# A two-layer hybrid decoder in split float32: p turns moved apart, low parts of the output weights in halves, first halves of the output product around the last head, and turns moved in the gated embedding

## What is computed

```python
for i in range(DEPTH):                                   # DEPTH = 2
    x = layer_norm(DN_ALPHA * x + 0.5 * swiglu(x, gate[i, 0], up[i, 0], down[i, 0]), ...)
    m = mixer_attention(...) if i % 2 == 0 else mixer_sgu(...)
    x = layer_norm(DN_ALPHA * x + m, ...)
    x = layer_norm(DN_ALPHA * x + 0.5 * swiglu(x, gate[i, 1], up[i, 1], down[i, 1]), ...)
    x = x + jax.nn.sigmoid(x @ ple_w_gate[i]) * (p[i] @ ple_w_proj[i])
# mixer_attention: h = x @ w_in; 8 heads with a relative-position bias and 8 "forgetting" heads
# (logits + c_t - c_s, c = cumsum(log_sigmoid(f))); softmax; o = concat(heads); return o @ w_out
```

## Time and profile before

| | us |
|---|---|
| median of three runs (1066.32 to 1066.38) | 1066.37 |
| profiled execution | 1067.42 |
| its span | 1065.1 |
| TensorE busy | 1033.4 |
| VectorE busy | 611.2 |
| ScalarE busy | 449.7 |
| POOL busy | 39.2 |

### The profile page before, as it was taken

The page is one execution under the profiler, slowest core; times in us unless marked ns, Lnnn a source line. Parts: engine busy times, 40 slices in busy tenths (PEclk is TensorE's granted clock), DMA queues, the critical chain, the costliest instruction groups (busy, mean ns, idle before and its releaser), DMA issues.

```text
span 1065.1 us, 12659 instructions
## 1 busy us (share of the span) xinstructions
PE 1033.4 (97%) x4770; PEld 845.3 (79%) x4770; DVE 611.2 (57%) x706; ACT 449.7 (42%) x523; POOL 39.2 (4%) x53
## 2 busy tenths in 40 slices
PE   7999999999998899999998999999999899999998
PEld 6888888777877688888886888888887688888886
DVE  5645455874455855445576554545677775454574
ACT  5434444245444443434435344344344354444441
POOL 2000000100000100000010000000110100000010
PEclk9999999999998999999999999999999999999999
DMA  8865655445133585565636755556267575655531
GB/s 287 280 203 184 203 189 167 136 142 157 40 103 111 184 275 197 160 205 182 201 105 219 261 181 180 197 159 208 87 207 237 174 261 188 206 187 168 197 119 40
DMA packets 129218, 191.46 MB, mean 180 GB/s; under 512 B 5368, under 2 KB 95480, under 8 KB 129056
## 3 DMA queue, kind: packets, MB, share of 16 engines
q1 hardware_dynamic: 126256, 180.37, 51.4%
q0 software_dynamic: 2928, 10.61, 3.0%
HBM read 189.90 MB, written 1.06 MB: 179 GB/s over the span
## 4 chain that ended last, share of the span: by engine, by line
PE 88%; DVE 4%; DMA 3%; ACT 2%; issue 2%; SPq 0%; POOL 0%; ACTq 0%; DVEq 0%
PE gu L358 19%; PE gu L360 18%; PE gu L359 18%; PE acc L358 9%; PE acc L360 9%; PE acc L359 9%; PE tp L416 4%; DVE g_lo L992 1%; ACT g_hi L742 1%; PE acc L561 1%; DMA rawB<-in_ffn_w_up 1%; DMA v_att<-bias_rows 1%; DMA rawB<-in_sgu_w_out 1%; DVE xT_lo L992 1%; DMA ws_tok<-in_sgu_w_s 0%
## 5 line engine op out<-in xcount | busy, mean ns | idle before, releaser
L358 PE MATMUL gu<-g_hi,xT_hi 128*128 128x512 f32 x928 | 365.3, 394 | 7.7 <-DVE xT_lo L992 7.5
L360 PE MATMUL gu<-g_hi,xT_lo 128*128 128x512 f32 x928 | 362.3, 390 | 0.0
L359 PE MATMUL gu<-g_lo,xT_hi 128*128 128x512 f32 x928 | 361.9, 390 | 0.0
L358 PEld LDWEIGHTS gu<-g_hi,xT_hi 128*128 128x128 f32 x928 | 174.7, 188 | 45.8 <-DVE xT_lo L992 7.4
L360 PEld LDWEIGHTS gu<-g_hi,xT_lo 128*128 128x128 f32 x928 | 174.6, 188 | 36.7
L359 PEld LDWEIGHTS gu<-g_lo,xT_hi 128*128 128x128 f32 x928 | 174.8, 188 | 35.6 <-issue 0.2
L791 ACT ACTIVATE stage<-gu 128x256 f32<-128x256 f32 x88 | 33.8, 384 | 380.1 <-PE gu L360 380.1
L992 DVE TENSOR_TENSOR g_lo<-rawA,g_hi 128x2048 fp32r<-128x2048 f32 (+1 forms) x64 | 143.4, 2240 | 82.9 <-ACT g_hi L742 82.9
L992 DVE TENSOR_TENSOR g_lo<-rawB,g_hi 128x2048 fp32r<-128x2048 f32 (+1 forms) x64 | 143.1, 2237 | 25.1 <-ACT g_hi L742 25.1
L1091 DVE SCALAR_TENSOR_TENSOR stage<-stage,gu 128x256 f32<-128x256 f32 x88 | 37.0, 421 | 197.0 <-ACT stage L791 197.0
L358 PE MATMUL acc<-d_hi,hT_hi 128*128 128x512 f32 x352 | 144.4, 410 | 0.0
(11 more groups left out here) (167 smaller groups left out, 682.8 us busy)
## 6 DMA issues: line engine op xcount, KB each, us to landing
rawD<-in_ffn_w_down SPq DMA_DIRECT2D x44, 1024.0 KB, 4.9
rawA<-in_ffn_w_gate SPq DMA_DIRECT2D x43, 512.0 KB, 4.0
rawA<-in_ffn_w_up SPq DMA_DIRECT2D x43, 512.0 KB, 5.0
rawB<-in_ffn_w_gate SPq DMA_DIRECT2D x43, 512.0 KB, 4.2
rawB<-in_ffn_w_up SPq DMA_DIRECT2D x43, 512.0 KB, 5.4
rawA<-in_attn_w_in SPq DMA_DIRECT2D x12, 512.0 KB, 4.6
rawB<-in_attn_w_in SPq DMA_DIRECT2D x12, 512.0 KB, 4.7
rawA<-in_ple_w_gate SPq DMA_DIRECT2D x8, 512.0 KB, 4.7
```

Of the source, the lines that this page charges most:

```text
L358: pe.matmul(dst, hi[b], w_hi[b], start=first and b == 0, stop=False)
L359: pe.matmul(dst, hi[b], w_lo[b], start=False, stop=False)
L360: done = pe.matmul(dst, lo[b], w_hi[b], start=False, stop=last and b == len(hi) - 1)
```

## The change

Four edits, made together.

- ATTN_ORDER: p turn 0 goes ahead of k's turn ("turn", 1, 1), p turn 1 behind the product ("g", 3, 0), ahead of head 0, on every engine.
- Heads: VectorE's two low parts of 4 blocks of the output weights become four of 2 blocks, in heads 12 to 15 behind the logits, each for the high part that ScalarE made a head earlier; a semaphore `out_high_front` tells of the first halves. On TensorE the probabilities' turn goes ahead of the attention result's turn; ScalarE's and VectorE's steps for that turn move from heads 16 and 17 to heads 15 and 16.
- Output product: the first part of (0, 0) runs ahead of head 17 (the last values), the first part of (0, 1) behind it; then both oT turns, and the loop does only second parts for j = 0. VectorE makes the low part of the next load (`lo_g(g0 + 8, 0)`) ahead of the xT_lo of turn 0, and that of the FFN's first half (`lo_g(g0 + 9, 0)`) ahead of the second residual of half 0. ScalarE's high part for it waits for `out_front_done` in place of the end of (0, 1).
- Gated embedding of layer 0: TensorE does the half-1 turns six products before the end of product 1, and product 2 in two parts, each behind its own bank. ScalarE does half 1's high parts ahead of sigmoid 1 and the high part of the next load ahead of sigmoid 2, behind `ple_front_done`. VectorE does half 1's low parts behind the first gate product. In the FFN behind it ScalarE and VectorE do half 1 ahead of the weights' parts of the next chunk.

```diff
@@ -55,13 +55,14 @@
...
 ("g", 1, 0), ("turn", 0, 1), ("exp",), ("g", 1, 1), ("turn", 1, 0), ("log",),
-("g", 2, 0), ("turn", 1, 1), ("pT", 0), ("pT", 1), ("g", 2, 1), ("cT",),
-("g", 3, 0), ("head", 0), ("g", 3, 1), ("turn", 3, 0), ("head", 1), ("head", 2),
+("g", 2, 0), ("pT", 0), ("turn", 1, 1), ("g", 2, 1), ("cT",),
+("g", 3, 0), ("pT", 1), ("head", 0), ("g", 3, 1), ("turn", 3, 0), ("head", 1), ("head", 2),
 ("g", 4, 0), ("turn", 3, 1), ("head", 3), ("head", 4),
...
 ("g front", 5, 1), ("head", 9), ("g back", 5, 1), ("head", 10),
-] + [("head", n) for n in range(HEADS + 3, 2 * HEADS + 2)] + [("oT", 0), ("oT", 1)]
+] + [("head", n) for n in range(HEADS + 3, 2 * HEADS + 1)] + [
+("out front", 0), ("head", 2 * HEADS + 1), ("out front", 1), ("oT", 0), ("oT", 1)]

@@ -251,6 +252,8 @@
...
 proj_full, proj_taken = sem("proj_full"), sem("proj_taken")
+out_high_front, out_front_done, ple_front_done = (
+sem("out_high_front"), sem("out_front_done"), sem("ple_front_done"))
 ws_loaded, vn_ready, mix_done, sgu_bias_ld, ws_raw = (
@@ -524,14 +527,25 @@
...
                 pe.wait_ge(act_done, a0 + n - 1)
-            if n % 2 == 0:
+            if n == 0 or n == 2 and i == 1:
                 xT_wait(h, use)
...
                 ln_turn(0, x0, (t0, t0 + 1))
-            g_product(g0 + j, (g0 + j) % 2, h, gu[j][:, :])
-            if n == 1:
+            if n == 1 and i == 0:
+                for part, ks in ((0, 4), (1, 6)):
+                    pe.wait_ge((split_a, split_b)[part], g0 + j)
+                    g_piece((g0 + j) % 2, h, gu[j][:, :], 4 * part, ks)
                 half1()
+                g_piece((g0 + j) % 2, h, gu[j][:, :], 6, KB).then_inc(g_done, 1)
+            elif n == 2 and i == 0:
+                for part in range(2):
+                    pe.wait_ge(tp_taken[part], use[h] + 1)
+                    done = g_piece((g0 + j) % 2, h, gu[j][:, :], 4 * part, 4 * part + 4)
+                    done.then_inc((ple_front_done, g_done)[part], 1)
+            else:
+                g_product(g0 + j, (g0 + j) % 2, h, gu[j][:, :])
             if n == 1 and i == 1:
+                half1()
                 d_product(d0, d0 % 2, 0, pT_hi[:, 0], pT_lo[:, 0], first=True, last=True)
@@ -648,6 +662,8 @@
...
                     scores(n)
+                if 1 <= n <= 2 * HEADS:
+                    probs_turn(n - 1)
                 if n in (15, 16):
@@ -655,30 +671,29 @@
...
                     done.then_inc(o_turned, 1)
-                if 1 <= n <= 2 * HEADS:
-                    probs_turn(n - 1)
                 if n >= 2:
...
                     proj(n - PROJ_AT)
+            elif e[0] == "out front":
+                h = e[1]
+                pe.wait_ge(o_split, h + 1)
+                if h == 0:
+                    pe.wait_ge(split_a, g0 + 7)
+                done = g_piece((g0 + 7) % 2, h, acc[h][:, 0, :], 0, 4)
+                if h == 1:
+                    done.then_inc(out_front_done, 1)
+            elif e[0] == "oT":
+                h = e[1]
+                pe.wait_ge(tok_ready, x0 + 2 + h + 1)
+                transposes(tp_of[e][0], t0 + tp_of[e][1],
+                           [t_tok[:, h, 512 + P * q:512 + P * q + P] for q in range(4)])
         out0, y_turn = g0 + 7, None
...
         def y_wait(j, h):
-            if j == 0:
-                pe.wait_ge(o_split, h + 1)
-            else:
-                bank, at = tp_of[("oT", h)]
-                pe.wait_ge(tp_taken[bank], t0 + at + 1)
-
-        def y_rest():
-            for h in range(HALVES):
-                bank, at = tp_of[("oT", h)]
-                pe.wait_ge(tok_ready, x0 + 2 + h + 1)
-                transposes(bank, t0 + at,
-                           [t_tok[:, h, 512 + P * q:512 + P * q + P] for q in range(4)])
-            y_wait(0, 1)
-            g_piece((g0 + 7) % 2, 1, acc[1][:, 0, :], 0, 4)
+            bank, at = tp_of[("oT", h)]
+            pe.wait_ge(tp_taken[bank], t0 + at + 1)

@@ -715,8 +730,6 @@
...

-        y_rest = None
-
         def y_wait(j, h, use=use):
@@ -728,8 +741,8 @@
...
             g_product(out0 + j, (out0 + j) % 2, h, acc[h][:, j, :],
-                      y_wait if n % 2 == 0 else None, y_rest if n == 0 else None,
-                      (1,) if n == 2 and y_rest is not None else (0, 1))
+                      y_wait if n % 2 == 0 else None, None,
+                      (1,) if j == 0 and kind == "attn" else (0, 1))
         use = after
@@ -794,8 +807,10 @@
...
                 half1()
+            if cs == 0 and k > 0 and PHASES[k - 1][0] == "ple":
+                half1()
             hi_g_into(c + (g0 + 1), slot, 0)
-            if k > 0 and cs == 0:
+            if cs == 0 and k > 0 and PHASES[k - 1][0] != "ple":
                 half1()
@@ -843,14 +858,17 @@
...
         for n, (j, h) in enumerate(PAIR):
-            if n == 2:
+            if n == 2 - (i == 0):
                 half1()
+            if n == 2 and i == 0:
+                act.wait_ge(raw_a, 32 * (g0 + 2))
+                act.wait_ge(ple_front_done, 1)
+                copy(g_hi[:, g0 % 2, 0:4, :], rawA[:, :, :]).then_inc(high_a, 1)
             act.wait_ge(g_done, 2 * g0 + n + 1)
...
             if n == 2 and not last_phase:
-                hi_g(g0 + 2, 0)
                 xT_high(0, t0)
@@ -920,10 +938,9 @@
...
                     done = hi_rows(g0 + 7, part, slice(2 * rows, 2 * rows + 2))
-                    if rows == 1:
-                        done.then_inc((high_a, high_b)[part], 1)
-                if n in (16, 17):
-                    h = n - 16
+                    done.then_inc((out_high_front, (high_a, high_b)[part])[rows], 1)
+                if n in (15, 16):
+                    h = n - 15
                     act.wait_ge(o_turned, h + 1)
@@ -933,7 +950,14 @@
...
         hi_g(g0 + 8, 1)
-        after, end = g0 + 9, t0 + 6 + HEADS + 1
+        end = t0 + 6 + HEADS + 1
+
+        def hi_after():
+            act.wait_ge(raw_a, 32 * (g0 + 9))
+            act.wait_ge(out_front_done, 1)
+            copy(g_hi[:, (g0 + 9) % 2, 0:4, :], rawA[:, :, :]).then_inc(high_a, 1)
+            xT_high(0, end)
+            hi_g(g0 + 9, 1)

@@ -967,12 +991,15 @@
...
         xT_high(1, t0)
-        after, end = g0 + 6, t0 + 2
+        end = t0 + 2
+
+        def hi_after():
+            hi_g(g0 + 6, 0)
+            xT_high(0, end)
+            hi_g(g0 + 6, 1)

     if kind in ("attn", "sgu"):
-        hi_g(after, 0)
-        xT_high(0, end)
-        hi_g(after, 1)
+        hi_after()

@@ -1097,12 +1124,10 @@
...
                 gated(c, 0)
-            if k == 0 and cs == 0:
+            if cs == 0 and light:
                 half1()
...
             if cs == 0 and light:
-                if k > 0:
-                    half1()
                 gated(c, 0)
@@ -1161,7 +1186,7 @@
...
             lo_d(d0, d0 % 2)
-        low_1()
+            low_1()
         for n, (j, h) in enumerate(PAIR):
@@ -1175,6 +1200,8 @@
...
                 .then_inc(tok_ready, 1)
+            if n == 0 and i == 0:
+                low_1()
             if n == 2 and not last_phase:
@@ -1290,10 +1317,20 @@
...
                     group_out(0, (n - HEADS - 2,))
-                if n in (PROJ_AT + 1, PROJ_AT + 3):
-                    lo_g(g0 + 7, (n - PROJ_AT - 1) // 2)
-                if n in (16, 17):
-                    h = n - 16
+                if PROJ_AT < n <= PROJ_AT + 4:
+                    part, rows = (n - PROJ_AT - 1) // 2, (n - PROJ_AT - 1) % 2
+                    if rows == 0:
+                        dve.wait_ge(out_high_front, part + 1)
+                    else:
+                        dve.wait_ge((high_a, high_b)[part], g0 + 7)
+                    ks = slice(4 * part + 2 * rows, 4 * part + 2 * rows + 2)
+                    done = low(g_lo[:, (g0 + 7) % 2, ks, :],
+                               (rawA, rawB)[part][:, 2 * rows:2 * rows + 2, :],
+                               g_hi[:, (g0 + 7) % 2, ks, :])
+                    if rows == 1:
+                        done.then_inc((split_a, split_b)[part], 1)
+                if n in (15, 16):
+                    h = n - 15
                     dve.wait_ge(o_hi, h + 1)
@@ -1302,9 +1339,8 @@
...
                     group_out(1)
+                    lo_g(g0 + 8, 0)
                 xT_low_block(1, h, v0 + 1, bank=1 - h)
-                if h == 0:
-                    lo_g(g0 + 8, 0)
         lo_g(g0 + 8, 1)
@@ -1366,11 +1402,14 @@
...
         residual(0, 0, r0, (g_done, 2 * out0 + 1))
+        if kind == "attn":
+            lo_g(out0 + 2, 0)
         ln_moments(0, residual(0, 1, r0, (g_done, 2 * out0 + 2)))
...
         residual(1, 0, r0, (g_done, 2 * out0 + 3))
-        lo_g(out0 + 2, 0)
+        if kind == "sgu":
+            lo_g(out0 + 2, 0)
         xT_low(0, end)
```

## The result

The changed kernel took 1052.47 us in the median of 8 runs (1051.58 to 1061.03), the kernel before 1066.34 beside it; the ratio is 0.9883, with a 95% interval of 0.986 to 0.9907. Forecast were 1053.8 and 1051.6 to 1056.8. In the runs at a mean granted clock of 0.999 to 1.000 the time was 1051.6 to 1052.0, at 0.998 it was 1053.0 to 1053.7, and the one at 0.990 took 1061.0.

A forecast was written before the change was run, and what follows sets the result against it. TensorE, busy 1033.4 of 1065.1 us, was taken as the bound. Gains 4.1 + 5.0 + 5.0 = 14.1 from 1067.42 gave 1053.3, 1052.3 on the median's scale; plus 1.5 for one clock fall, 1053.8, range 1051.6 to 1056.8.

The forecast's parts named there:

- The p turns: Attention projections: the 2.52 us wait and 1.55 of half-speed clock behind it go, 4.1 us; bounds 2.5 to 4.4.
- The halves: Last heads: low parts in halves avoid VectorE's waits; 5.1 us of TensorE waits become 1.5, and 2.95 of clock returns.
- The fronts: Output product's first halves around the last head: new 1.25 us wait for xT_lo, residual 0.35 us late.
- parts 2 and 3: Last heads' halves and output product's fronts, priced together: 5.3 us gained by the end of (1, 0), clock included.
- The gated embedding: Gated embedding and FFN behind it: waits of 1.72, 1.06 and 1.51 us for xT_lo go; 5.0 us gained.
- tight points: Gated embedding: half-1 turns fit by 0.17 us; the next chunk's other half is ready with 0.6 us to spare.
- The tail together: Last heads, output product and FFN start: 5.3 - 0.35 + 0.1 = 5.0 us gained, before a possible clock fall costing 1.5.
- The clock: Between scores 15 and the first wide product, narrow work makes the clock fall once, losing 1.5 us; chance 0.45.
- Clock holds: Rival: the clock does not fall in the tail, since waits there are short; 1052.3 us; chance 0.25.
- The slower rival: The clock falls at head 11 and stays at 1.2 GHz through the last heads; 1073 us; chance 0.02.
- Loads take the place of the waits: Rival: late loads delay the residual and keep the gated embedding's last gap; typically 1055.5, at most 1057.1 us; chance 0.20.
- doesn't do what it says: Rival: long wait stays, only the p turns and the gated embedding's first gap are won; 1060.4 or 1062 us; chance 0.05.

The follow-up runs named there:

- e1: The kernel before with only the p turns moved apart; 1063.85 us against 1066.53 beside it, ratio 0.998.
- e7: The changed kernel with the output weights' low parts whole again and the attention result's turns in their old places; 1060.75 us against 1053.83.
- e6: The changed kernel with the low part of the first FFN half back behind the residuals; 1053.17 us against 1053.83.
- e9: The kernel before with 19 unused products of 512 columns filling the 4.41 us wait at head 16; 1064.41 us against 1065.94, ratio 0.9986.
- e5: The changed kernel without the output product's fronts and with the two low parts moved forward for them put back; 1050.59 us against 1053.83.
- e8: The changed kernel again, unaltered, on the same chip as three variants of it; 1053.83 us in 7 runs.
- e10: The kernel before with 40 unused turns of 128 columns filling the 4.41 us wait at head 16; 1064.76 us against 1065.94, ratio 0.999.
- e12: The changed kernel without the output product's fronts, run once more; 1053.12 us in six runs.
- e2: The kernel before with only the heads part: low parts in halves, probabilities turned first, attention result turned a head earlier; 1059.79 us against 1066.53, ratio 0.9945.
- e11: The changed kernel without the output product's fronts, plus unused products filling the waits for the normalisation; 1050.25 us against 1053.12 without the filling.
- e4: The kernel before with only the gated embedding's part and the FFN behind it; 1061.37 us, ratio 0.9953.
- e3: The kernel before with only the output product's fronts and the two low parts moved forward; 1070.15 us, ratio 1.0036.

## Why the prediction held, point by point

**1. The p turns.** Right in mechanism and size in the trace: 4.1 forecast, 4.38 - 0.2 measured. As a median of many runs it is nearer to its lower bound of 2.5: e1 gained 2.7.

**2. The halves.** Right: no low part waits for ScalarE's second half, and the waits 0.70 and 4.41 became 0.52 and 0.31, where 0.8 and 0.5 were forecast. The 0.2 us wait for the attention output's low part didn't come. The clock's share was too large: 2.95 forecast, 2.1 measured with the wait filled. Whether the halves would do it without the earlier turns was not run; that VectorE's wait of 4.18 us comes back with the long wait in e7 speaks for the halves.

**3. The fronts.** The waits were foreseen: 1.25 for xT_lo, measured 0.97; the residual 0.35 late, measured 338.03 against 337.79 in e6, 0.24 (1.46 against the forecast 1.7 in TensorE's wait). The 0.1 us that the early low part was to save behind the FFN's start didn't come: the wait there is 1.62, before 1.46. The failed step is that parts 2 and 3 were priced in one chain, 5.3 us up to the end of (1, 0), and the fronts never against the halves alone. With stretches in which the clock held, B is 63.58 in the old order (e9, whose filling is as long as the wait), 58.62 with the halves (e5) and 60.32 with the fronts added (e8). So the halves by themselves are worth 5.0 us at full clock and 2.1 of clock where it fell; the fronts take 1.7 of it back. The working had all that was needed. It had the values moved behind front 0, the normalisation behind the values, and nothing wide left between the turns and their low part. Set beside a chain with the old order, it would have shown a loss.

**4. The gated embedding.** Right: 5.0 forecast, 5.3 in C. All three waits of the earlier trace rows are gone, no late load shows as a wait of TensorE, and the tight points (0.17 and 0.6 us) held.

**The tail together.** Forecast were 5.0, with the 2.95 of clock loss before given back, and 3.5 with one new fall. B lost 65.69 - 60.32 = 5.4 in e8's profile, where the clock held, and 65.69 - 61.76 = 3.9 in the first one, with one fall. Of either, 63.58 - 60.32 = 3.3 is waits and work at full clock; the rest is the 2.1 us of clock given back, less 1.4 for the new fall in the first. That the forecast of 5.0 is so near is partly luck: the clock's share was put 0.8 too high, the waits left in the last heads 0.7 too high (1.5 against 0.52 + 0.31).

**The clock.** One fall was forecast, and the profile has one, at the right price (1.49 by the estimate, 1.44 against e8). Its place and its reason were wrong. It should have come in the narrow work between scores 15 and the first wide product; there the clock was 1.00 in this profile and in e8's. It came behind the waits of 1.46 and 0.79 us for the normalisation. The premise that turns don't hold the clock fell with e10.

**The rivals.** "Clock holds" (1052.3) is what half of the runs did, with 1051.6 to 1052.0; the other four took 1053.0 to 1061.0. The median of 1052.47 is the middle between the two groups, so that it speaks for neither. The slower rival, a clock that falls at head 11 and stays low through the last heads, was put at 0.02 for all runs to come out at 1073. Its mechanism is real but partial and only in some executions. Where the trace has it, the fall is in the scores of head 11 as put, but it lasted 6.8 or 13.7 us and cost 3.1 or 6.2, not 21. The chance was set for every run at once, and the event comes in single ones. "Loads take the place of the waits" and "doesn't do what it says" did not occur.

**The number.** For the profiled execution with one fall the forecast comes to 1053.3 + 1.5 = 1054.8, and it took 1052.98. Of the 1.8 us between them A has 0.1, B 0.4 and C 0.3; the other 1.0 lies outside what was changed, 0.7 of it ahead of A. In the median the miss is 1.3 us.

## What to carry to other kernels

Price every edit against the version without it, also where several edits lie in one chain: two edits that together gain 5.4 us can be one of 7.1 and one of -1.7. Before wide work is moved ahead of narrow work to fill a wait, ask what it was covering where it stood and what now starts later behind it. A wait costs its length and, in some executions, up to half of the work that follows at 0.50: 2.1 us behind the 4.41 us wait here, 1.4 to 1.6 or nothing behind the one of 2.52 us. The second share belongs in the range rather than in the sum, unless every execution shows it.

## What the runs showed of the hardware that was not expected

The clock can fall where TensorE has not waited for some 40 us. In the trace of e12 the last idle time of TensorE over 0.25 us ahead of it is at 257.7, and the clock is low from 300.7 on; windows over heads 9 to 11, the projection quarter behind them included:

```profile
292.00:300.70 8.70, 8.70 (x47) 6.48 (x45) 3.97 (x15) 3.57 (x10) 0.00 (x0) 1.00 0.15 34
300.70:307.50 6.80, 6.80 (x21) 5.15 (x21) 2.50 (x11) 3.00 (x9) 0.00 (x0) 0.50 0.32 120
```

The same was in e2 (304.7 for 13.7 us) and e11 (302.1 for 13.7 us), and in no profile of the other eleven. The records show TensorE busy for the whole of the stretch ahead. All three times it is in the scores of head 11, which follow head 10 with no wide product between the two; that this mix is the reason is a guess. The falls seem more frequent with the halves in: three of seven profiles of kernels with them have one, none of seven without. Of the executions, 10 of 44 of kernels with them were more than 5 us above their kernel's fastest, and 8 of 114 of kernels without, though a total doesn't tell where the clock fell. Why is open, since the halves' first instruction that differs stands behind the fall. No run here took the work of these heads apart.

The clock's answer to one and the same wait was not fixed either. Behind the 2.52 us in A it fell in before, e2, e4 and e10, and held in e3 and e9.
